# Expert items 1 to 6 of TensorE's program written out instead of looped

## The chip, the cores and the metric

One core of one Trainium2 chip runs the whole program. The metric is the device time of one execution in microseconds (us). The time before is the median of three runs, 1470.57 us (1469.07 to 1472.14).

## What is computed

The reference is a small model on 256 tokens of width 1024: two layers of a convolution and gating mixer, the first followed by a dense SwiGLU, the second by a mixture of 8 SwiGLU experts (each 1024 to 2816 to 1024, two experts a token), then an attention block with two kinds of attention. The change lies in the experts:

```python
D_MODEL = 1024; D_FF = 2816; N_EXPERTS = 8; TOP_K = 2

def swiglu(h, wg, wu, wd):
    return jnp.einsum('...f,fd->...d', jax.nn.silu(h @ wg) * (h @ wu), wd)

def moe_swiglu(h, router, wg, wu, wd):
    ...
    logits = jnp.einsum('td,de->te', ht, router).astype(jnp.float32)
    top_vals, top_idx = lax.top_k(logits, TOP_K)
    gates = jax.nn.softmax(top_vals, axis=-1)
    ...
    for e in range(N_EXPERTS):
        out = out + dense_gate[:, e:e + 1] * swiglu(ht, wg[e], wu[e], wd[e])
```

The expert weights are float32: 3 x 1024 x 2816 x 4 bytes, 34.6 MB for one expert, 277 MB for all eight.

## The kernel before, in words

Every engine runs one instruction stream of its own, and the streams are tied by semaphores. The program is the mixer of layer 0, the dense SwiGLU, the mixer of layer 1, the router, then the **items**, and then the attention block. An item is up to 96 tokens of one expert. There are at least 8, numbered 0 to 7 (`NE` is 8), and up to five more when an expert is crowded; the number of the last one is known only on the chip (`last`, read from `plan`).

An item's weights are cut into 24 chunks. Chunks 0 to 15 are gate and up weights: 0 to 7 are 1.57 MB each, 8 to 15 are 1.31 MB each. Chunks 16 to 23 are the down weights, 1.57 MB each, the last two 1.05 MB. They land in a ring of 8 slots (`ering`, `ESLOTS` is 8). SyncE issues their DMAs (`load_expert`, line 452): the DMA of chunk c waits until TensorE is done with chunk c - 8 (semaphore `w_used`), since that is the one whose slot it takes. TensorE waits for a chunk by the semaphore `e_landed` of its slot. So up to seven whole chunks can be on their way or landed while TensorE works on one.

TensorE multiplies by all of a chunk in one go: the tokens (`xe`) or the hidden values (`eT`) are the stationary side, 32 columns of them at a time, one after the other on four column strips (`by_strips`, line 2701), and the weights stream through. In the trace, a `LDWEIGHTS` and a `MATMUL` record stand for each half of a product in float32. After chunk 8 and chunk 16 TensorE turns the hidden values of one half (`turn_hidden`, line 2687), and after chunk 16 also the tokens of the next item (`turn_tokens`, line 2680). VectorE and ScalarE do the activation, the product with the up part and the copies, with waits that count up by fixed steps each item. ScalarE writes an item's result to `ys` with three DMAs, and SyncE reads the next item's tokens from `xs` with one.

On each of the four engines the items are written alike: item 0 by itself, then a hardware loop over items 1 to 6, then a branch over a second, conditional body for items beyond the eighth, then the last item by itself. Inside the loop the item number i is a register, so the values that the waits compare with are worked out in registers (`landed(i, j)`, `FREED * i` and the like). The function `item` tells item 0 from the looped ones by `isinstance(i, int)`: item 0 waits for other semaphores on its first four chunks, reads `last`, and turns the places of the last item's tokens.

Of the kernel before, what the change touches and what calls it, by code (L numbers as in the profile page):

```python
# [34 lines left out]
NE = 8  # L35
# [91 lines left out]
def model_program(nc, a, out):  # L127
# [313 lines left out]
    def landed(i, j):  # L441

        slot = range(j % ESLOTS, FFN_CHUNKS, ESLOTS)
        before = 16 * MOE0 // RAWS if slot[0] < RAWS else 0
        return before + 16 * sum(LANDINGS[n] for n in slot if n <= j) + i * (16 * sum(LANDINGS[n] for n in slot))
# [705 lines left out]
    def second_tensor(pe, n_items, norm_transposes, last_item):  # L1151
# [22 lines left out]
        def meta_low(c):  # L1174
            pe.wait_ge(blo_made, c + 1)
            _, wl = wide(c)
            for k in range(4):
                kt = 4 * c + k
                mm = nc.tensor.matmul(ps[0:META, 3, 0:W2], xTm_hi[:, kt, T:TM], wl[:, k, :], start=False, stop=kt == KT - 1)
            return mm  # L1180
# [352 lines left out]
    with nc.Block() as block:  # L1533
# [807 lines left out]
        def _(pe):  # L2341
# [333 lines left out]
            def turn_tokens(i):  # L2675
                pe.wait_ge(xg_landed, 16 * (i + 1))
                for part in range(2):
                    for kk in range(4):
                        k = 4 * part + kk
                        mm = nc.tensor.transpose(ps[:, part, kk * CAP:kk * CAP + CAP], xg[0:CAP, k * P:k * P + P], ident[0:CAP, 0:CAP])  # L2680
                    mm.then_inc(tp_filled, 1)

            def turn_hidden(i, piece):
                pe.wait_ge(emult_made, MULTS * i + (7 if piece else 3))
                for jb in range(3):
                    for t in range(TOKS):
                        mm = nc.tensor.transpose(ps[:, 3 + jb, t * P:t * P + P], eh[piece][:, t, jb * P:jb * P + P], ident)  # L2687
                    mm.then_inc(tp_filled, 1)

            def turn_last_places():  # L2690
                pe.wait_ge(pick_made, 2 + TOKS * NB)
                for t in range(TOKS):
                    for b in range(NB):
                        first = (2 * (t % 2) + b) * P
                        mm = nc.tensor.transpose(ps[:, 6 + t // 2, first:first + P], pick_last[:, t, b, :], ident)
                mm.then_inc(g0_filled, 1)
# [7 lines left out]
            def gate_or_up(j):  # L2704
                piece, up = j // 8, j // 4 % 2
                n = WIDE[piece]
                w = slot_view(ering, j % ESLOTS, 2, STRIPS * n)
                for k in range(2):
                    kt = 2 * (j % 4) + k
                    for t in range(TOKS):  # L2710
                        mm = by_strips(lambda rows: ps[rows, 3 * up + t, 0:n], xe[:, kt, STRIP * t:STRIP * t + STRIP], w[:, k, :], n,
                                       kt == 0, kt == KT - 1)
                return mm

            def down(j, t, n, tile):
                w = slot_view(ering, j % ESLOTS, len(DOWN_TILES[j - 16]), D)
                first = t % 2 * DOWN_N
                return by_strips(lambda rows: ps[rows, 6 + t // 2, first:first + DOWN_N], eT[:, tile, STRIP * t:STRIP * t + STRIP],
                                 w[:, n, :], DOWN_N, tile == 0 and t != 1, tile == FT - 1)

            def item(i, last=False):
                first = isinstance(i, int)
                for j in range(16):
                    if first and j < 4:
                        pe.wait_ge(g0_hi if j % 2 else g0_freed, j // 2 + 1)
                    if j == 0 and not first:
                        pe.wait_ge(tp_freed, FREED * i)
                        pe.wait_ge(esilu_made, 7 * i)
                    if j == 8:
                        pe.wait_ge(esilu_made, 7 * i + 3)  # L2730
                    if j == 12:
                        pe.wait_ge(tp_freed, FREED * i + 3)
                        if first:
                            read_last()
                    pe.wait_ge(e_landed[j % ESLOTS], landed(i, j))
                    gate_or_up(j).then_inc(w_used, 1)
                    if j == 8:
                        turn_hidden(i, 0)
                        if first:
                            turn_last_places()  # L2740
                for j in range(16, FFN_CHUNKS):
                    if j == 16 and first:
                        pe.wait_ge(g0_freed, 4)
                    elif j == 16:
                        pe.wait_ge(eo_made, 2 * i)
                    if j == 20:
                        pe.wait_ge(tp_freed, FREED * i + 7)
                    pe.wait_ge(e_landed[j % ESLOTS], landed(i, j))
                    if last and j == FFN_CHUNKS - 1:
                        for t in range(TOKS):  # L2750
                            for n, tile in enumerate(DOWN_TILES[j - 16]):
                                mm = down(j, t, n, tile)
                            if t:
                                mm.then_inc(w_used if t == TOKS - 1 else acc_ready, 1)
                        return
                    for n, tile in enumerate(DOWN_TILES[j - 16]):
                        for t in range(TOKS):
                            mm = down(j, t, n, tile)
                    mm.then_inc(w_used, 1)
                    if j == 16:  # L2760
                        turn_hidden(i, 1)
                        if not last:
                            turn_tokens(i)
# [3 lines left out]
            def read_last():  # L2767
                pe.wait_ge(routed, 1)
                last_of.append(pe.value_load(plan[0:1, LAST_COL:LAST_COL + 1], min_val=NE - 1, max_val=ITEMS - 1))

            pe.wait_ge(pick_made, 2)
            for p in range(4):
                gather(p)
            item(0)
            with pe.Fori(1, NE - 1) as i:
                item(i)
            last = last_of[0]
            n_items = last + 1
            with pe.If(last > NE - 1):
                with pe.Fori(NE - 1, ITEMS - 1) as i:  # L2780
                    with pe.If(i < last):
                        item(i)
# [38 lines left out]
```

## Time and profile before

| what | us |
|---|---|
| median of three runs | 1470.57 |
| the profiled execution, its own time | 1468.36 |
| its span in the trace | 1466.5 |
| TensorE busy in it | 1393.0 (95%) |
| VectorE, ScalarE, GpSimd busy | 514.8, 384.8, 75.2 |

The span runs from the first to the last instruction in the trace; the 1.9 us between it and the execution's time lie around it. The eight items take roughly from 407 to 1187 us. The rows of the section below come from this one execution. In a chain or a timeline, the first number is the start in us from the span's start, the second the length. A granted clock (PEclk) of 1.00 is TensorE at 2.4 GHz, 0.50 is 1.2 GHz.

### The profile page before, as it was taken

What the parts mean: (1) busy time and instruction counts of PE and PEld (TensorE: products, weight loads), DVE (VectorE), ACT (ScalarE), POOL (GpSimd) and SP (SyncE); (2) the same over time, 40 slices, a digit from 0 to 9 for tenths busy, and PEclk for the clock granted to TensorE, in tenths of its full rate; (3) what the DMA queues carried; (4) which work ended last, traced back from release to release, by engine and by line L of the source; (5) the groups of instructions that cost most, each with busy time, mean ns of one, the idle gap of its engine ahead of it and who ended that gap; (6) DMA issues with size and microseconds to landing.
All of it is one profiled execution on the core that took longest, in us unless ns stands there. A gap on an engine that the chain in (4) does not pass through costs nothing.

```text
span 1466.5 us, 33021 instructions
## 1 busy us (share of the span) xinstructions
PE 1393.0 (95%) x14972; PEld 960.6 (66%) x14972; DVE 514.8 (35%) x836; ACT 384.8 (26%) x527; POOL 75.2 (5%) x130
## 2 busy tenths in 40 slices
PE   6999999999999999798997997998989989999998
PEld 6879998897855656245354453452554559788896
DVE  6975555389522001010010010010101154656665
ACT  5664443346400000000000000000000045656653
POOL 3400000043010000000000000000000010000000
PEclk9999999999899999899998998998999999999999
DMA  9569974454779999999999999999999955343341
GB/s 320 162 219 328 294 230 171 144 178 152 312 297 357 382 390 348 382 358 345 370 351 366 343 347 378 341 374 336 344 353 403 353 205 169 104 143 117 116 169 61
DMA packets 122585, 407.35 MB, mean 278 GB/s; under 512 B 7430, under 2 KB 35958, under 8 KB 122436
## 3 DMA queue, kind: packets, MB, share of 16 engines
q1 hardware_dynamic: 114192, 389.57, 74.7%
q0 software_dynamic: 5408, 12.58, 2.6%
q8 instruction: 133, 2.18, 0.6%
q10 hardware_dynamic: 2836, 2.88, 0.6%
q14 instruction: 16, 0.13, 0.0%
HBM read 396.78 MB, written 16.12 MB: 282 GB/s over the span
## 4 chain that ended last, share of the span: by engine, by line
PE 84%; DVE 8%; issue 4%; ACT 2%; DMA 1%; SPq 0%; DVEq 0%; ACTq 0%
PE ps L2701 48%; PE ps L516 6%; PE ps L518 6%; PE ps L517 6%; DVE yT L2027 3%; PE ps L1198 1%; DVE low L506 1%; PE ps L1200 1%; PE ps L1199 1%; PE ps L2687 1%; PE ps L2386 1%; DMA rawb<-in_w_in 1%; PE ps L1407 1%; PE ps L1405 1%; PE ps L1406 1%
## 5 line engine op out<-in xcount | busy, mean ns | idle before, releaser
L2701 PE MATMUL ps<-ering,xe 128*32 128x384 f32 (+1 forms) x6144 | 481.4, 470 | 43.4 <-issue 43.4
L2701 PEld LDWEIGHTS ps<-ering,xe 128*32 128x32 f32 x6144 | 213.8, 112 | 306.0 <-issue 186.6
L2701 PE MATMUL ps<-ering,eT 128*32 128x256 f32 x4224 | 233.0, 379 | 2.0 <-issue 2.0
L2203 DVE TENSOR_TENSOR eh<-eh,ps 128x384 f32<-128x384 f32 (+1 forms) x48 | 22.1, 517 | 580.3 <-PE ps L2701 580.3
L2701 PEld LDWEIGHTS ps<-ering,eT 128*32 128x32 f32 x4224 | 146.5, 110 | 84.9 <-issue 3.4
L506 DVE TENSOR_TENSOR low<-raw,high 128x2048 fp32r<-128x2048 f32 (+3 forms) x48 | 128.9, 2686 | 61.6 <-ACT high L501 60.4
L501 ACT ACTIVATE high<-raw 128x2048 fp32r<-128x2048 f32 (+3 forms) x47 | 105.5, 2246 | 91.0 <-PE ps L518 76.1
L516 PE MATMUL ps<-high,xT_hi 128*128 128x352 f32 (+1 forms) x368 | 128.2, 348 | 1.2 <-DVE xT_lo L2109 1.2
L518 PE MATMUL ps<-high,xT_lo 128*128 128x352 f32 (+1 forms) x368 | 127.1, 345 | 0.0
L1880 ACT ACTIVATE eh<-ps 128x384 f32<-128x384 f32 (+1 forms) x48 | 18.9, 466 | 411.8 <-PE ps L2701 411.8
L517 PE MATMUL ps<-low,xT_hi 128*128 128x352 f32 (+1 forms) x368 | 126.9, 345 | 0.0
L903 DVE TENSOR_TENSOR lowb<-rawb,highb 128x2048 fp32r<-128x2048 f32 x35 | 80.0, 2289 | 47.7 <-ACT highb L681 47.6
L681 ACT ACTIVATE highb<-rawb 128x2048 fp32r<-128x2048 f32 x35 | 66.9, 1911 | 84.8 <-DMA rawb<-in_w_in 38.2
L1890 ACT ACTIVATE eo<-ps 128x512 f32<-128x512 f32 x8 | 4.8, 596 | 298.5 <-PE ps L2701 298.5
L516 PEld LDWEIGHTS ps<-high,xT_hi 128*128 128x128 f32 x368 | 69.1, 188 | 7.7 <-DVE xT_lo L2109 2.2
L518 PEld LDWEIGHTS ps<-high,xT_lo 128*128 128x128 f32 x368 | 69.2, 188 | 5.1
L517 PEld LDWEIGHTS ps<-low,xT_hi 128*128 128x128 f32 x368 | 69.2, 188 | 4.8
L1198 PE MATMUL ps<-xTm_hi,highb 128*128 128x256 f32 x224 | 64.2, 286 | 0.0
L1199 PE MATMUL ps<-xTm_lo,highb 128*128 128x256 f32 x224 | 62.6, 279 | 0.0
L1200 PE MATMUL ps<-xTm_hi,lowb 128*128 128x256 f32 x224 | 62.5, 279 | 0.0
L2027 DVE SCALAR_TENSOR_TENSOR yT<-cT,cols,yT 128x256 f32<-128x256 f32 x120 | 48.8, 480 | 0.0
L1198 PEld LDWEIGHTS ps<-xTm_hi,highb 128*128 128x128 f32 x224 | 42.1, 188 | 1.3 <-issue 1.2
(436 smaller groups left out, 1670.5 us busy)
## 6 DMA issues: line engine op xcount, KB each, us to landing
ering<-in_moe_wg SPq DMA_DIRECT2D x32, 1536.0 KB, 15.7
ering<-in_moe_wu SPq DMA_DIRECT2D x32, 1536.0 KB, 17.6
ering<-in_moe_wd SPq DMA_DIRECT2D x32, 1536.0 KB, 11.9
ering<-in_moe_wg SPq DMA_DIRECT2D x32, 1280.0 KB, 9.2
ering<-in_moe_wu SPq DMA_DIRECT2D x32, 1280.0 KB, 8.5
rawb<-in_w_in SPq DMA_DIRECT2D x25, 1024.0 KB, 5.1
ering<-in_moe_wd SPq DMA_DIRECT2D x24, 1024.0 KB, 17.1
raw<-in_w_in SPq DMA_DIRECT2D x16, 1024.0 KB, 9.1
```

The costliest lines, as they stand in the source:

```text
L501: nc.scalar.activation(high[:, c % SPLITS, 0:n], raw[:, c % RAWS, 0:n], ACT.Copy).then_inc(hi_made, 1)
L506: nc.vector.tensor_tensor(low[:, c % SPLITS, 0:n], raw[:, c % RAWS, 0:n], f(high[:, c % SPLITS, 0:n]), ALU.subtract).then_inc(lo_made, 1)
L516: nc.tensor.matmul(out, xh, wh, start=first, stop=False)
L517: nc.tensor.matmul(out, xh, wl, start=False, stop=False)
L518: return nc.tensor.matmul(out, xl, wh, start=False, stop=last)
L681: nc.scalar.activation(highb[:, c % SPLITS, :], rawb[:, c % RAWSB, :], ACT.Copy).then_inc(bhi_made, 1)
L903: nc.vector.tensor_tensor(lowb[:, c % SPLITS, :], rawb[:, c % RAWSB, :], f(highb[:, c % SPLITS, :]), ALU.subtract).then_inc(blo_made, 1)
L1198: nc.tensor.matmul(o, wh[:, k, chans], yT_hi[:, kt, :], start=kt == 0 and t == 0, stop=False, **mmx)
L1199: nc.tensor.matmul(o, wh[:, k, chans], yT_lo[:, kt, :], start=False, stop=False, **mmx)
L1200: mm = nc.tensor.matmul(o, wl[:, k, chans], yT_hi[:, kt, :], start=False, stop=kt == KT - 1, **mmx)
L2027: ins = nc.vector.scalar_tensor_tensor(yT[:, t, :], src, w, yT[:, t, :], ALU.mult, ALU.add)
L2701: mm = nc.tensor.matmul(out_of(rows), tokens, weights[:, n * s:n * s + n], start=begins, stop=ends, skip_group_check=True)
```

## The change

TensorE's loop over items 1 to 6 becomes a Python loop, so that six bodies stand one behind the other in its program with plain constants in their waits. The test for "first" is narrowed, since now six more items are called with an int. VectorE, ScalarE and SyncE keep their hardware loops, and the conditional second loop of TensorE stays as it is.

```diff
             def item(i, last=False):
-                first = isinstance(i, int)
+                first = isinstance(i, int) and i == 0
                 for j in range(16):
...
             item(0)
-            with pe.Fori(1, NE - 1) as i:
+            for i in range(1, NE - 1):
                 item(i)
             last = last_of[0]
```

```order
 L2680 MATMUL ps<-small,xg 128x96 x8
 L2701 MATMUL ps<-ering,eT 32x256 x228
-L2775 UNCONDITIONAL_BRANCH
-L2775 ISA
-L2728 REGISTER_ALU
-L2735 ISA
-L2701 MATMUL ps<-ering,xe 32x384 x96
-L2735 ISA
-L2701 MATMUL ps<-ering,xe 32x384 x48
-L2735 REGISTER_ALU
-L2701 MATMUL ps<-ering,xe 32x384 x48
```

The branch into the loop's head and the sequencer's register work at the head are gone; the same 192 products follow the 228 of item 0 directly (next block).

At the loop's end, the closing branch goes and another item begins in its place:

```order
-L2775 REGISTER_ALU
-L2775 COMPARE_AND_BRANCH
+L2701 MATMUL ps<-ering,eT 32x256 x228
+L2701 MATMUL ps<-ering,xe 32x384 x192
+L2701 MATMUL ps<-ering,xe 32x320 x24
+L2687 MATMUL ps<-small_68,eh_113 128x128 x9
+L2701 MATMUL ps<-ering,xe 32x320 x168
+L2701 MATMUL ps<-ering,eT 32x256 x36
```

The compare and branch that closed the loop stands nowhere in the new program; the branch at L2779, over the conditional body, stays where it was, behind item 6. On SyncE and ScalarE no instruction differs between the two programs.

## Rows read from the trace of the kernel before

**Rows 1.** The page: TensorE's busy time, and the span in 40 slices.

```profile
PE 1393.0 (95%) x14972; PEld 960.6 (66%) x14972; DVE 514.8 (35%) x836; ACT 384.8 (26%) x527; POOL 75.2 (5%) x130
...
PEclk9999999999899999899998998998999999999999
DMA  9569974454779999999999999999999955343341
GB/s 320 162 219 328 294 230 171 144 178 152 312 297 357 382 390 348 382 358 345 370 351 366 343 347 378 341 374 336 344 353 403 353 205 169 104 143 117 116 169 61
```

**Rows 2.** Chain of waits in time, 500 to 1150 us: start, length, what.

```profile
577.58 0.72 issue
...
587.57 5.08 issue
592.65 2.76 PE ps L2701 x10
595.41 2.50 issue
597.91 35.79 PE ps L2701 x419
...
1090.80 5.29 issue
1096.09 5.22 PE ps L2701 x33
```

**Rows 3.** Waits: SyncE's queue, 500 to 1190 us; TensorE, 500 to 1150 (total, times, longest).

```profile
SPq L452 <- PE ps L2701: 544.1, 159, 16.2
...
PE ps L2701 <- issue: 45.1, 14, 5.3
```

**Rows 4.** Timeline of TensorE, the first products of item 1.

```profile
497.50 0.49 PE L2701 MATMUL ps<-ering,xe 128*32 128x384 f32 x2
```

**Rows 5.** Windows at two edges: PE, PEld, DVE, ACT, POOL busy, PEclk, DMA, GB/s.

```profile
587.60:602.10 14.50, 6.95 (x38) 1.94 (x42) 0.00 (x0) 0.88 (x2) 0.00 (x0) 0.65 1.02 414
...
1090.80:1100.70 9.90, 4.61 (x32) 1.51 (x33) 0.00 (x0) 0.87 (x2) 0.00 (x0) 0.66 1.02 413
```

**Rows 6.** DMA view, 350 to 1170 us: the instruction queue, tokens, results.

```profile
q8 instruction: 98, 1.61, 0.8%
...
xg<-xs SPq DMA_DIRECT2D x7, 384.0 KB, 11.4
ys<-eo ACTq DMA_DIRECT2D x21, 128.0 KB
```

**Rows 7.** Windows of an item's length or so, same columns as rows 5.

```profile
483.00:580.00 97.00, 96.28 (x1461) 57.96 (x1455) 7.18 (x16) 3.46 (x9) 0.00 (x0) 1.00 1.02 380
498.00:587.60 89.60, 88.85 (x1320) 50.78 (x1312) 7.18 (x16) 3.46 (x9) 0.00 (x0) 1.00 1.02 377
...
677.00:776.00 99.00, 90.62 (x1309) 46.58 (x1305) 7.18 (x16) 3.46 (x9) 0.00 (x0) 0.98 1.01 366
...
1081.00:1174.00 93.00, 87.30 (x1250) 43.21 (x1252) 11.21 (x18) 3.46 (x9) 5.04 (x8) 0.96 0.98 382
```

**Rows 8.** Time from issue to landing, expert chunks issued 537 to 588 us.

```profile
DMA to landing us min/median/max: 13.8/20.9/24.5
```

**Rows 9.** The same, chunks issued 990 to 1041 us.

```profile
DMA to landing us min/median/max: 5.7/7.5/10.8
```

**Rows 10.** Windows within item 1 and its end, same columns as rows 5.

```profile
498.00:540.00 42.00, 42.00 (x543) 23.54 (x539) 2.97 (x6) 2.13 (x5) 0.00 (x0) 1.00 1.02 415
...
567.00:579.00 12.00, 11.28 (x213) 6.71 (x205) 0.00 (x0) 0.00 (x0) 0.00 (x0) 1.00 1.02 246
```

**Rows 11.** The DMA of item 2's chunk 1, alone in the window 565 to 566 us.

```profile
L452 SPq DMA_DIRECT2D ering<-in_moe_wg x1: 372/372/372, 565.9 to 565.9; - x1
...
DMA to landing us min/median/max: 20.9/20.9/20.9
```

**Rows 12.** Chain of waits, 985 to 1190 us: what follows the last item.

```profile
1175.35 12.28 DMA rawb<-in_w_in
...
1189.53 0.59 ACT eo L1890
```

## The prediction

> **What bounds the kernel now.** I read the page first. TensorE is busy 95% of the span, so the end is set by what it does and where it stands still. But in slices 13 to 32, the items, the DMA engines are busy nine tenths or more as well and move 336 to 403 GB/s, and the granted clock dips to 8 tenths in several slices [rows 1]. So two resources are near their limits, and a pause taken out of one can run into the other.
>
> The chain of waits on TensorE shows the pauses. At 587.57, where item 1 ends and item 2 begins, TensorE stands for 5.08 us, does ten matmuls, stands another 2.50 us, and goes on; the wait is put down to "issue", to nothing that the profile can name, not to a DMA or an engine [rows 2]. The same pair comes behind items 2, 3, 4 and 5, and behind item 6 a single pause of 5.29 us [rows 2]. Together these are 45.1 us of "issue" in 14 pieces, TensorE's only wait in that stretch [rows 3]. All the long ones sit where the loop branches back or is left; at the entry of item 1 there is none, its first products begin at 497.50 [rows 4]. I read them as the fetch of TensorE's code after a jump: one item is some 2,630 instructions (1320 matmuls and 1312 weight loads in its 89.6 us [rows 7]), and the second pause, ten matmuls in, has the look of the next piece of code being late too.
>
> The pauses also cost clock. In the 14.5 us from 587.6 the mean granted clock is 0.65, against 1.00 over item 1 [rows 5, 7]: TensorE falls from 2.4 to 1.2 GHz after standing, and comes back after some microseconds of work.
>
> The Trainium skill, "Runtime: NRT & Kernel Launch", section "Instruction fetch mechanics", says that instructions are fetched in order ahead of use and that a taken branch to a place outside what is held makes the engine wait for a fetch. The trace agrees, with 5.08 us at the branch and none at the straight entry of item 1.
>
> Last, how far ahead the weights are. SyncE's queue waits for TensorE to free a slot for 544.1 us in all [rows 3], which looks as if DMA had time to spare. The time to landing says otherwise: 20.9 us in the median for chunks issued from 537 to 588 us, 24.5 at most [rows 8], and only 7.5 for those issued from 990 to 1041 [rows 9]. An item of 24 chunks takes TensorE about 90 us, 3.8 a chunk, so seven chunks of lead are some 26 us, and that is all there is. In item 1, which had no pause in front of it, the DMA was falling behind; after each pause it had caught up. The pauses give the DMA time.
>
> **What the change takes away.** Five taken branches, behind items 1 to 5. From the end of item 1 (587.57) to the end of item 6 (1090.80) are 503.2 us for five items, 100.6 us each [rows 2]. Item 1 itself, without a pause ahead, took 587.57 - 497.50 = 90.1 us [rows 2, 4]. The difference, 10.5 us an edge, is 5.1 + 2.5 = 7.6 us of pauses and 2.9 us for the lower clock. If nothing else held, five items would take 450.5 us, and **52.7 us** would go.
>
> **What is late next.** The weights. An item needs 34.6 MB of them, 0.39 MB of tokens and 3 x 0.13 MB of results [rows 6], and 1.61 MB of instructions over about eight items, 0.2 each [rows 6]: 35.6 MB. The DMA does 415 GB/s through gate and up chunks but only 246 GB/s at the end of an item, where the down weights land in strips [rows 10]. Over windows of about one item with many chunks under way it did 380, 377 and 382 GB/s, and 366 in a window where it was less far behind [rows 7]. A period of the DMA alone is therefore 35.6 / 0.382 = 93.2 us at best, 35.6 / 0.366 = 97.3 us at worst. Both are above TensorE's 90.1. In the changed kernel the DMA has all eight slots to work on, which speaks for the upper rates, but TensorE's waits come where landing is slowest, which the windows may flatter: their edges cut through chunks that have partly landed. I take the middle of 380 and 366, 373 GB/s, so 95.4 us.
>
> How much lead is left at 587.57: item 2's chunk 1 was issued at 565.9 and landed 20.9 us later, at 586.8 [rows 11]. Without a pause TensorE wants it one chunk after 587.57, at 591.4. The lead is 4.6 us and lasts for less than one item (95.4 - 90.1 = 5.3). From then on, an item takes the DMA's time, and item 7's chunk 1 lands five periods after item 2's, just when it is wanted. The five items take 5 x 95.4 - 4.6 = 472.4 us instead of 503.2: **30.8 us less.** With 93.2 it is 41.8, with 97.3 it is 21.3.
>
> **What I cost at nothing.** The register work and the branch into the loop: before, they showed as no pause at item 1's entry [rows 4]; below that there is only the gap's own size. Straight code crosses fetches too; in item 1 that showed once, 0.72 us [rows 2]. At one such pause for each of five items that would be 3.6 us if TensorE were the bound; waiting for weights, it hides them, so zero, with 3.6 as the far end. The branch behind item 6 stays. It cost 5.29 us and a clock of 0.66 for a while [rows 2, 5]; its place among the fetched pieces of code shifts, so a second pause of 2.5 us may appear, as behind the others [rows 2], or the present one shrink, by 5.3 at most. I take no change. Behind it item 7 goes on as before: the pause gives the DMA some 8 us, and item 7's window needed 382 GB/s [rows 7], which is what the DMA can do. After item 7 the attention block's first weights are on the chain, issued at 1175.35 [rows 12]. They are issued when TensorE frees slots, so they move with it; should the backlog reach them, their landing slips by no more than the lead lost, 4.6 us. None is taken, both ends go to the range.
>
> **The sum.** Profiled execution: 1468.4 - 30.8 = 1437.6 us. The median of the runs is 2.2 us above that execution, so **1440 us**, rounded.
>
> **The rivals.**
> *The DMA keeps up* (TensorE remains the bound). For it: 415 GB/s over 42 us [rows 10]; if the slow end of an item is smoothed by a deep queue, 35.6 / 0.415 = 85.8 us, under 90.1. Against: in item 1 the queue was deep and the end ran at 246 all the same. Time: 1470.6 - 52.7 = 1418 us. Chance 0.13.
>
> *The DMA's limit is lower than I think* and the pauses were mostly cover for it. For it: with the pauses, slices 18 to 29, items 2 to 6, drew only 336 to 378 GB/s [rows 1]. A rate of 358 GB/s would make the period 99.4 us, five items 492.4, the gain 10.8, the time 1460 us. Against: 380 GB/s over 97 us [rows 7]; the lower slices have landing times down to 5.7 us [rows 9], so the DMA was then waiting for slots. The Trainium skill, "DMA: Bandwidth & Descriptors", section "Specifications", gives 358 GB/s as the HBM limit of a core and 435 as the fabric's ceiling; by the first this rival would be right, and the trace, with one core at work, is above it. Chance 0.17.
>
> *Slower: the clock.* Starved of weights, TensorE would wait at the slow end of every item, fall to 1.2 GHz, and pay more than the loop did. One fall costs 2.9 us, as at an edge. An item is longer than before once it has 10.5 / 2.9 = 3.6 falls; with five, it takes 104.6 us, five items 20 us more than before, 1490 us. For it: at 246 GB/s [rows 10] a last chunk of 1.05 MB takes 4.3 us to land, and TensorE two thirds of 3.8, 2.5 us, to use, which leaves gaps of 1.8 us. Against: the pause of 0.72 us left the clock of item 1 at 1.00 [rows 7], the falls came after 5 us; and a slow TensorE no longer waits for the DMA, so it fills its time again and recovers. The Trainium skill, "TensorE: Matmul & The Clock Gate", section "HAM oscillation — how this bites in real kernels", describes such a kernel, in which each wait for weights let the clock drop again; no run here shows that. Chance 0.04.
>
> *It does not do what it says*: the long pauses are not of the branch but of something each item start has, and stay. Against: item 1's start has none. 1470.6 us, chance 0.03.
>
> **How the numbers follow.** The forecast, period 93.2 to 97.3 us, has 0.63, its own range 1429 to 1450. Lower, the DMA-keeps-up case adds 0.13 down to 1418; upward, half of the lower-limit case lies between 1450 and 1460. The range is 1418 to 1460. About 0.2% (3 us) is what a measurement can tell from no change. Faster by more than that: forecast, keeps-up and lower-limit cases, 0.93. Within: 0.03. Slower: 0.04.
>
> **What would show it.** At the edges of items 1 to 5 no "issue" pause over 1 us, and no dip in clock there. Behind item 6 a pause of about 5 us still. Item 2 some 90 us long, items 4 to 6 some 95 us. TensorE waiting for landed chunks at the end of items, a few microseconds an item. Landing times of 20 us and more in the median throughout, and 370 to 380 GB/s in every item. I am wrong if items 4 to 6 take 90 us (the DMA keeps up), if they take 99 or more (its limit is lower), or if the clock over them is under 0.9 (the clock).

## The result, and the profile after

The median went from 1470.23 us (7 runs, 1466.16 to 1472.14) to **1458.26 us** (7 runs, 1455.77 to 1464.85): a ratio of 0.9931, 95% interval 0.9909 to 0.9953. That is 12 us less, clear of what a measurement can tell from no change, inside the range of the prediction, and 39% of the 30.8 us that it forecast.

The page of the changed kernel, the lines that answer to [rows 1]:

```profile
PE 1385.4 (95%) x14972; PEld 960.7 (66%) x14972; DVE 514.8 (35%) x836; ACT 384.2 (26%) x527; POOL 75.0 (5%) x130
...
PEclk9999999999899999999999999999999989999999
DMA  9569864454879999999999999999999945243341
GB/s 321 163 223 327 295 227 173 144 174 155 315 296 365 379 390 336 415 376 336 407 314 372 382 288 413 375 321 407 327 381 377 319 165 179 96 144 116 116 174 58
```

The dips of the clock inside the items are gone, and yet TensorE's share is still 95%. The chain of waits of the changed kernel, from 480 to 700 us, shows the edges of items 1 (at 586.4) and 2 (at 677.1); it answers to [rows 2]:

```profile
560.27 16.10 PE ps L2701 x295
576.37 1.04 issue
577.41 43.20 PE ps L2701 x593
...
671.00 1.49 issue
672.49 4.62 PE ps L2701 x77
```

From 577.41 on TensorE works through the place at which it stood for 5.08 and 2.50 us before. Small pauses of the straight code remain, 1.04 and 1.49 us here, over the 1 us that the prediction allowed at an edge. TensorE's waits from 490 to 1090 us (total, times, longest) answer to [rows 3]:

```profile
PE ps L2701 <- DMA ering<-in_moe_wd: 21.7, 12, 2.8
PE ps L2701 <- issue: 7.6, 3, 5.1
PE ps L2701 <- DMA ering<-in_moe_wu: 4.7, 15, 0.4
PE ps L2701 <- DMA ering<-in_moe_wg: 3.4, 6, 0.9
PE ps L2680 <- DMA xg<-xs: 2.0, 3, 0.8
```

The 45.1 us of "issue" became 7.6, of which 5.1 is the pause behind item 6 that was to stay. In their place stand 31.8 us of waits for transfers, in 36 pieces, none longer than 2.8 us. The windows of items 1 to 6 (columns as in [rows 5]):

```profile
496.50:586.40 89.90, 88.86 (x1329) 49.05 (x1322) 7.18 (x16) 3.44 (x9) 0.00 (x0) 1.00 1.02 373
586.40:677.10 90.70, 89.18 (x1323) 54.90 (x1314) 7.18 (x16) 3.44 (x9) 0.00 (x0) 1.00 1.02 367
677.10:779.60 102.50, 93.91 (x1326) 46.28 (x1330) 7.18 (x16) 3.45 (x9) 0.00 (x0) 0.97 1.02 361
779.60:878.60 99.00, 91.99 (x1322) 44.79 (x1314) 7.18 (x16) 3.45 (x9) 0.00 (x0) 0.98 1.02 357
878.60:977.70 99.10, 90.93 (x1322) 44.91 (x1322) 7.18 (x16) 3.45 (x9) 0.00 (x0) 1.00 1.02 365
977.70:1077.00 99.30, 90.94 (x1322) 45.70 (x1322) 7.19 (x16) 3.44 (x9) 0.00 (x0) 1.00 1.01 367
```

Item 2 still takes TensorE's time, 90.7 us: the lead is used up in it. From item 3 on an item takes 99 us and more, hardly less than the 100.6 with the pauses, and the DMA engines are busy throughout, yet move only 357 to 367 GB/s. The times to landing, chunks issued from 677 to 728 us and from 728 to 777 (against 7.5 in the median in [rows 9]):

```profile
DMA to landing us min/median/max: 21.4/23.4/29.4
...
DMA to landing us min/median/max: 15.9/26.6/31.8
```

Within item 3 the windows say where the rate is lost (columns as before); they answer to [rows 10]:

```profile
677.10:732.00 54.90, 52.57 (x681) 23.07 (x685) 2.97 (x6) 3.45 (x9) 0.00 (x0) 1.00 1.02 410
732.00:750.00 18.00, 17.24 (x280) 9.88 (x273) 4.21 (x10) 0.00 (x0) 0.00 (x0) 1.00 1.03 358
750.00:774.00 24.00, 19.66 (x328) 11.14 (x320) 0.00 (x0) 0.00 (x0) 0.00 (x0) 0.93 1.03 245
774.00:800.00 26.00, 24.44 (x296) 9.46 (x300) 0.00 (x0) 2.13 (x5) 0.00 (x0) 0.93 1.01 410
```

The stretch at 245 GB/s, with the DMA engines as busy as elsewhere, is 24 us long; in item 1 of the kernel before, a window of 12 us showed 246. It is where the last down chunks and the first chunks of the next item are under way.

So the change did what it says, and the expected gain went into waits for weights. Two questions were open: is it only the weights, and why do they come at 99 us an item when 35.6 MB at 415 GB/s would take 86?

### The profile page after: what moved, and what is told of

Read it like the earlier page. It is cut to its first block, busy times and chain, and to the rows that moved or that the text cites. A ratio compares the mean times of both kernels' runs of the same rounds, so it can differ in the third digit from the quotient of the medians.

```text
span 1461.4 us, 32936 instructions
## 1 busy us (share of the span) xinstructions
PE 1385.4 (95%) x14972; PEld 960.7 (66%) x14972; DVE 514.8 (35%) x836; ACT 384.2 (26%) x527; POOL 75.0 (5%) x130
## 4 chain that ended last, share of the span: by engine, by line
PE 61%; DMA 21%; DVE 7%; SPq 7%; issue 2%; ACT 2%; ACTq 0%; DVEq 0%; POOL 0%; POOLq 0%
PE ps L2701 24%; DMA ering<-in_moe_wu 8%; PE ps L516 6%; PE ps L518 6%; SPq L452 6%; PE ps L517 6%; DMA ering<-in_moe_wd 5%; DMA ering<-in_moe_wg 4%; DVE yT L2027 3%; DMA ys<-eo 2%; PE ps L1198 2%; PE ps L1200 2%; PE ps L1199 2%; DVE low L506 1%; DMA rawb<-in_w_in 1%
## 5 line engine op out<-in xcount | busy, mean ns | idle before, releaser
L2701 PE MATMUL ps<-ering,xe 128*32 128x384 f32 (+1 forms) x6144 | 464.1, 461 | 13.2 <-issue 5.1
L2701 PE MATMUL ps<-ering,eT 128*32 128x256 f32 x4224 | 240.9, 385 | 25.9 <-DMA ering<-in_moe_wd 22.4
## 6 DMA issues: line engine op xcount, KB each, us to landing
ering<-in_moe_wd SPq DMA_DIRECT2D x32, 1536.0 KB, 21.9
```

Source lines behind the costliest of these rows:

```text
L2701: mm = nc.tensor.matmul(out_of(rows), tokens, weights[:, n * s:n * s + n], start=begins, stop=ends, skip_group_check=True)
```

## The experiments

Each experiment's ratio is to runs of the kernel before made beside it, with medians of 1469.4 to 1469.6 us. The straight kernel (the changed one) was not run again beside them; its 1458.26 us and its ratio of 0.9931 (0.9909 to 0.9953) come from the runs above. Where an edit changes how many DMAs load a chunk or store a result, the counts that the waits compare with change along; those lines are left out of the diffs.

### Halved loads, looped and straight

Both kernels with half of chunks 0 to 7 left out in items 1 to 7:

```diff
-            rows(slot_view(ering, s, 2, width), (wg_v, wu_v)[up][e, :, k:k + 2, piece * PIECE0:piece * PIECE0 + width])
+            count = 2 if piece or (isinstance(e, int) and e == 0) else 1
+            rows(slot_view(ering, s, 2, width)[:, 0:count, :],
+                 (wg_v, wu_v)[up][e, :, k:k + count, piece * PIECE0:piece * PIECE0 + width])
```

> The looped kernel with only half of chunks 0 to 7 loaded in items 1 to 7 (0.79 MB each instead of 1.57; the other half of each slot holds old data, so the expert products of those chunks are not the reference's). 34.6 MB an item become 28.3. If the loads bind the changed kernel: here, where the branch pauses bind, the items still take 100 to 101 us each, and the whole is 1470 us within 4. Rival (the loads also bind the looped kernel in part): 3 to 5 us an item shorter, below 1455 us.

> The same halved loads in the kernel with the items written out. If the landing of weights is what ate the gain: items 2 to 6 take TensorE's 90 us instead of 99, TensorE waits for no chunk, and the whole is 45 to 53 us under the looped kernel with halved loads, 1417 to 1425 us. Rival (the straight code itself is slower, by late fetches or by the clock): the items stay at 97 us or more, and the whole over 1450 us.

Measured: looped 1441.71 us (1438.46 to 1444.96; ratio to the kernel before 0.9812, 0.9776 to 0.9849), straight 1408.90 us (1407.78 to 1410.02; 0.9589, 0.9562 to 0.9616). In the straight kernel the items take 88.5 to 90.5 us at a clock of 1.00, with no wait for a chunk. These are the windows of its items 2 and 3:

```profile
584.40:672.90 88.50, 88.50 (x1326) 44.46 (x1322) 7.18 (x16) 3.45 (x9) 0.00 (x0) 1.00 0.95 330
672.90:761.60 88.70, 88.70 (x1329) 44.32 (x1325) 7.18 (x16) 3.45 (x9) 0.00 (x0) 1.00 0.95 330
```

With the landing relieved, the straight code runs at TensorE's own pace; the weights ate the gain. The straight kernel came out below the 1417 to 1425 us expected, and 33 us under the looped one instead of 45 to 53, since the looped one got faster too. That one missed its expectation, and the rival's sign came true: 28 us less, 20 of them in items 2 to 6, which take 96.5 us each instead of 100.6. Where the other 8 went was not taken apart. No wait for a chunk was removed there, since there was none. What shrank is the pause at the branch, in its chain of waits:

```profile
585.11 3.62 issue
588.73 1.47 PE ps L2703 x10
590.21 1.32 issue
...
680.23 3.95 issue
684.18 2.76 PE ps L2703 x10
686.95 0.17 issue
```

3.6 to 4.0 us and then 0.2 to 1.7 us, instead of 4.9 to 5.1 and 2.4 to 2.7: with fewer loads beside it (306 to 331 GB/s during the first pause instead of some 410), the late code comes sooner. The trace of the kernel before has the instruction queue's packets in both pauses, two in the first (587.6 to 592.7 us) and one in the second (595.4 to 598), 16 KB each:

```profile
q8 instruction: 2, 0.03, 2.9%
...
q8 instruction: 1, 0.02, 2.6%
```

All this fits a pause that is a transfer of code, sharing the DMA engines with the weights, so that the loop's price depends on them.

### The end chunk in one DMA, straight and looped

Chunk 23 holds the last 64 rows of each of the four strips, and is loaded by two DMAs, each onto 64 of the 128 partitions. Here it is one DMA of the same bytes:

```diff
-            ends = wd_v[e, PIECE0:, :].rearrange("(t u q) n -> u q t n", t=2, u=2)
-            for u in range(2):
-                rows(slot_view(ering, s, 2, D)[2 * STRIP * u:2 * STRIP * u + REST, :, :], ends[u, 2 * P:, :, :])
+            tiles(0, FF - 2 * P, 2)
```

> Straight kernel, chunk 23 loaded by one DMA onto all 128 partitions (the last 256 rows of the down weights, other rows than the reference's; same bytes) instead of two DMAs onto 64 partitions each. Theory A, second part (the loads onto a part of the partitions crowd the ways into them and slow what is beside them: GB/s falls to 250 at the end of an item): the rate there rises to over 380, items 3 to 6 take 94 to 95 us, the whole 16 to 20 us less, about 1440 us. Theory B (bytes alone): no change, 1458 within 4.

> The looped kernel with chunk 23 loaded by one DMA onto 128 partitions (other rows than the reference's, same bytes), the twin of the straight kernel with that load, which took 1406 us. If the loop's price is the branch pauses and the clock behind them, shown in full only where the loads don't bind: items 2 to 6 take 97 to 99 us (88.5 and 9 to 10 at the edge), the whole 1443 to 1455 us, so that straight against loop is worth 40 to 48 us here and was worth 12 with the split load. Rival (most of the 52 us that the whole load gave the straight kernel it gives the looped one too): under 1430 us.

Measured: straight **1406.07 us** (1403.04 to 1408.18; 0.9569, 0.9544 to 0.9595), far below the 1440 expected; looped 1464.07 us (1462.78 to 1465.62; 0.9968, 0.9958 to 0.9979), above the 1443 to 1455 expected. The windows of items 2 to 4 of the straight one:

```profile
583.70:672.20 88.50, 88.50 (x1326) 44.46 (x1322) 7.18 (x16) 3.44 (x9) 0.00 (x0) 1.00 1.02 398
672.20:760.70 88.50, 88.50 (x1326) 44.45 (x1322) 7.18 (x16) 3.44 (x9) 0.00 (x0) 1.00 1.02 402
760.70:849.20 88.50, 88.50 (x1326) 44.56 (x1322) 7.18 (x16) 3.44 (x9) 0.00 (x0) 1.00 1.02 400
```

About 400 GB/s over whole items, and TensorE never waits for a chunk: its period of 88.5 us is the bound, and this is the case "the DMA keeps up" of the prediction. The looped one keeps its edges, here in its chain of waits:

```profile
584.21 4.96 issue
589.18 2.76 PE ps L2699 x10
591.94 2.44 issue
...
682.43 5.07 issue
687.50 2.76 PE ps L2699 x10
690.26 2.71 issue
```

Its items take 98.2, 101.2, 100.2, 101.2 and 100.1 us, most of them more than the 97 to 99 expected: 88.5 us and some 11.7 for the edge and the clock behind it. **Writing out the items is worth 58 us with the whole load and 12 with the split one.** One part of the kernel held down what another could give. The two changes together bring 64 us, apart 12 and 5.

### The result stored by strips

ScalarE's three stores of an item have a target whose first dimension is 4, the strips. Here they are four stores of 32 partitions:

```diff
-                    for t in range(TOKS):
-                        act.dma_start(ys_v[i - 1, STRIP * t:STRIP * t + STRIP, :].rearrange("p (s n) -> s p n", s=STRIPS), eo[:, t, :]).then_inc(eo_landed, 16)
+                    for s in range(STRIPS):
+                        act.dma_start(ys_v[i - 1, :, DOWN_N * s:DOWN_N * (s + 1)].rearrange("(t p) n -> p t n", t=TOKS),
+                                      eo[STRIP * s:STRIP * s + STRIP, :, :]).then_inc(eo_landed, 16)
```

> Straight kernel, the item's result stored by four DMAs of 32 partitions each instead of three of 128 partitions whose target's first dimension is 4. Theory A (a chunk counts as landed when the slowest of the DMA engines is through; the stores put all their packets on four of the sixteen, which then land every chunk late, 4.4 us instead of 3.8 for chunks 3 to 7): chunks 3 to 7 land 3.8 us apart, items 3 to 6 take 96 us instead of 99, the whole about 12 us less, 1446 us. Theory B (the bound is the sum of bytes at some 360 GB/s, whatever engine carries them): no change, 1458 within 4.

Measured: 1451.57 us (1450.68 to 1454.71; 0.9887, 0.9863 to 0.9910), 7 us less than the straight kernel and not the 12 expected (the intervals of the two ratios just touch); items 3 to 6 take 100.3, 95.7, 99.3 and 94.7 us, 97.5 in the mean instead of 100.0. Chunks 3 to 7 land 4.0 us apart in the mean of these items, instead of 4.4. Theory B falls, since the bytes are the same. That the stores go over four engines shows in the DMA view of one item (583 to 671 us): queue 10 has 396 packets in the changed kernel and 448 here.

```profile
q10 hardware_dynamic: 396, 0.39, 1.3%
```

```profile
q10 hardware_dynamic: 448, 0.39, 1.3%
```

384 of them carry data; the rest are the marks with which each engine reports its share, 12 for three stores before, 64 for four now: 4 engines a store against 16. The Trainium skill, "DMA: Bandwidth & Descriptors", section "Why a DMA increments its semaphore by 16 and not by 1", says that the number of engines is the largest up to 16 that divides the slowest dimension of both sides. The trace agrees, 4 where that dimension is 4.

### Quarters by turns, and two queues

Two other ways to load chunk 23. In four DMAs, by turns from the lower and the upper half:

```diff
-            for u in range(2):
-                rows(slot_view(ering, s, 2, D)[2 * STRIP * u:2 * STRIP * u + REST, :, :], ends[u, 2 * P:, :, :])
+            for half in range(2):
+                for u in range(2):
+                    at = 2 * STRIP * u + STRIP * half
+                    rows(slot_view(ering, s, 2, D)[at:at + STRIP, :, :],
+                         ends[u, 2 * P + STRIP * half:2 * P + STRIP * half + STRIP, :, :])
```

> Straight kernel, chunk 23 correct, in four DMAs of 32 partitions each, taken by turns from the lower and the upper half of the partitions, instead of two of 64. Theory (a DMA onto 64 partitions has all sixteen engines write through half of the ways into the memory): by turns, engines that run apart would mix the halves, and the slow stretch at the end of an item gets faster; 1425 to 1445 us. Rival (small partial DMAs crowd whatever their order): 1458 us or more.

And with the second half on ScalarE's queue, behind the last activation of each item:

```diff
-            for u in range(2):
-                rows(slot_view(ering, s, 2, D)[2 * STRIP * u:2 * STRIP * u + REST, :, :], ends[u, 2 * P:, :, :])
+            rows(slot_view(ering, s, 2, D)[0:REST, :, :], ends[0, 2 * P:, :, :])
...
+            def second_ends(i, e):
+                s = (FFN_CHUNKS - 1) % ESLOTS
+                ends = wd_v[e, PIECE0:, :].rearrange("(t u q) n -> u q t n", t=2, u=2)
+                act.wait_ge(w_used, chunk(i, FFN_CHUNKS - ESLOTS))
+                act.dma_start(slot_view(ering, s, 2, D)[2 * STRIP:2 * STRIP + REST, :, :], ends[1, 2 * P:, :, :]).then_inc(e_landed[s], 16)
```

> Straight kernel, chunk 23 correct, its second half (64 partitions) issued on ScalarE's queue instead of SyncE's. It does not stand behind the other seven chunks there and is mixed packet by packet with loads onto all partitions. Theory as for the quarters: less crowding, 1430 to 1450 us. Rival: no change, 1458 us, or slower where ScalarE's wait for the slot delays the storing of a result.

Measured: quarters 1450.10 us (1448.20 to 1451.66; 0.9872, 0.9852 to 0.9891), 8 us less than the straight kernel, between the 1445 us of the theory and the 1458 of its rival; two queues 1458.08 us (1448.65 to 1461.35; 0.9908, 0.9878 to 0.9939), not to be told from no change. Neither the order nor the queue brings the 52 us that one DMA onto 128 partitions brings. It isn't the number of DMAs in a chunk either: four were no slower here than two, and chunks 20 and 21 are two DMAs each in every kernel, the 1406 us one too, but onto all partitions.

### A hint for the loop's branch

```diff
-            with pe.Fori(1, NE - 1) as i:
+            with nc.Fori(1, NE - 1, engines=[pe.engine], hint_back_edge=True) as i:
```

Measured: 1460.87 us (1456.99 to 1467.92; 0.9946, 0.9929 to 0.9962). The time is in the expected place, but the edges are not as expected. Its chain of waits:

```profile
587.18 4.21 issue
591.39 2.12 PE ps L2701 x9
593.51 3.26 issue
...
687.77 3.40 issue
691.17 2.12 PE ps L2701 x9
693.29 3.23 issue
```

The first pause falls from about 5.0 us to between 2.5 and 4.2, the second grows from about 2.5 us to between 3.2 and 3.5. The loads had been expected to become the bound, and did not: TensorE waits for no chunk in this run. That a hint about the fetch alone moves the pauses speaks for the fetch as their cause; why it takes away only a part is open. Nothing was tried on when the hinted code is asked for.

### Everything that the loads need, with the whole reference computed

The end rows of two neighbouring strips can be made 128 rows in a row, if the odd strips give up their first 64 columns instead of their last:

```diff
-            return PIECE0 + WIDE[1] * n
+            return PIECE0 + WIDE[1] * n + REST * (n % 2)
...
-            ends = wd_v[e, PIECE0:, :].rearrange("(t u q) n -> u q t n", t=2, u=2)
-            for u in range(2):
-                rows(slot_view(ering, s, 2, D)[2 * STRIP * u:2 * STRIP * u + REST, :, :], ends[u, 2 * P:, :, :])
+            ends = wd_v[e, PIECE0:, :].rearrange("(t r) n -> r t n", t=2)
+            rows(slot_view(ering, s, 2, D), ends[2 * P:3 * P, :, :])
...
+                def at(rows):
+                    return REST if piece and rows.start // STRIP % 2 == 0 else 0
...
-                        mm = by_strips(lambda rows: ps[rows, 3 * up + t, 0:n], xe[:, kt, STRIP * t:STRIP * t + STRIP], w[:, k, :], n,
+                        mm = by_strips(lambda rows: ps[rows, 3 * up + t, at(rows):at(rows) + n], xe[:, kt, STRIP * t:STRIP * t + STRIP], w[:, k, :], n,
```

Even strips write their 320 outputs from column 64 on, odd strips from 0; the activations read columns 64 to 383 and, for the ends, 0 to 63. No instruction is added.

> Straight kernel in which chunk 23 is one DMA onto 128 partitions and the whole reference is computed: odd strips give the first 64 of their 320 columns to the last tiles instead of the last 64, so that the ends of two neighbouring strips are 128 rows in a row. No instruction is added on TensorE. As in the run that loaded other rows in one DMA: items of 88.5 us, TensorE waits for no chunk until item 6, 1406 us within 4. Rival (what that run gained came from the place of its rows in memory, not from the shape of the DMA): over 1425 us.

The second kernel adds the stores by strips, the third loads the tokens onto 128 partitions instead of 96:

```diff
-                sp.dma_start(xg[0:CAP, :], xs_v[i + 1, :, :]).then_inc(xg_landed, 16)
+                sp.dma_start(xg[:, :], xs[bass.ds((i + 1) * CAP, P), :]).then_inc(xg_landed, 16)
```

> The same, with the results stored by four DMAs of 32 partitions. Theory A: the spread between the first and the last engine's share of a chunk no longer grows from item to item, chunks 3 to 7 land 3.8 us apart throughout, the loads run ahead of TensorE; since TensorE already bounds the items, the whole is at most 3 us less than without it, 1403 to 1406 us. Rival: the four extra stores an item cost something where item 7 begins, over 1408 us.

> The same, and the tokens loaded onto 128 partitions instead of 96 (32 rows more, which nothing uses). If loads onto a part of the partitions crowd: the interval of chunk 17 falls from 7 to under 5.5 us; hidden by the lead, so no change in the whole beyond 2 us, 1402 to 1406 us. Rival: the extra bytes cost, over 1408 us.

> The looped kernel with all three changes of the loads and stores, the twin of the run before. If the branch pauses are all that the loop costs: items 2 to 6 take 98 to 101 us, the whole 1455 to 1465 us, so that writing out the items is worth 52 to 58 us here. Rival (the relieved DMA engines also shorten the fetch pauses, as with the halved loads): pauses of 4 us instead of 5, the whole 1440 to 1455 us.

| kernel | median us | range | ratio to the kernel before (95%) |
|---|---|---|---|
| straight, ends in one DMA | 1405.73 | 1404.05 to 1406.49 | 0.9566 (0.9547 to 0.9585) |
| and stores by strips | 1402.26 | 1401.79 to 1406.85 | 0.9553 (0.9529 to 0.9577) |
| and tokens onto 128 partitions | 1405.92 | 1403.92 to 1406.27 | 0.9564 (0.9546 to 0.9583) |
| looped, with all three | 1466.01 | 1463.17 to 1467.87 | 0.9977 (0.9965 to 0.9989) |

The first meets the run with other rows (1406.07 us), so it was the shape of the DMA, not the place of its rows. This is the version that beats both kernels. The stores and the tokens on top make no difference that these runs can tell: TensorE is the bound. The interval at which chunk 17 lands behind chunk 16 was 5.3 to 7.0 us with the stores by strips and 4.2 to 4.7 with the tokens on 128 partitions, as expected (items 2 to 6). The first kernel's waits of TensorE, 490 to 1090 us, and its windows of items 3 and 6:

```profile
PE ps L2700 <- issue: 5.0, 1, 5.0
PE ps L2686 <- DVE eh L2202: 2.1, 1, 2.1
```

```profile
672.20:760.70 88.50, 88.50 (x1330) 44.47 (x1326) 7.18 (x16) 3.46 (x10) 0.00 (x0) 1.00 1.02 399
...
937.60:1026.10 88.50, 88.02 (x1318) 44.07 (x1310) 7.18 (x16) 3.44 (x10) 0.00 (x0) 1.00 1.02 401
```

Only the pause behind item 6 and one wait of 2.1 us for VectorE are left. The looped twin lies 60 us above the straight one, a little over the 52 to 58 expected, and its first pauses are 5.1 to 5.5 us long, so its rival with shorter ones did not come true.

Each of a chunk's sixteen shares has its landing in the trace. How far apart the first and the last of them are, in us, for chunk 4:

| kernel | item 3 | item 6 |
|---|---|---|
| before | 4.3 | 3.6 |
| straight | 9.8 | 13.3 |
| straight, stores by strips | 8.1 | 15.3 |
| straight, ends in one DMA (whole reference) | 4.4 | 9.5 |
| and stores by strips | 4.6 | 8.5 |
| and tokens onto 128 partitions | 2.7 | 3.2 |

TensorE can begin a chunk only when its last share is there. In the straight kernel the engines drift apart from item to item, until the first is 13 us ahead of the last; in the looped kernel before, the spread at these two items is about 4 us. The ends in one DMA narrow it, and the tokens on top of them bring it down to 3.2 us at item 6. The stores by strips had been expected to stop its growth, and did not: with the ends in one DMA it is 8.5 us at item 6, and in the straight kernel 15.3, though that kernel got 7 us shorter. A wide spread alone does not make an item slow: with the ends in one DMA it is 9.5 us at item 6, and the item takes 88.5.

Where the time goes shows in how long the last shares of a stretch of chunks take to come, in us, mean of items 3 to 6:

| kernel | chunks 0 to 2 | 3 to 7 | 8 to 15 | 16 to 23 | all 24 |
|---|---|---|---|---|---|
| straight | 11.4 | 21.9 | 26.7 | 40.0 | 100.0 |
| straight, stores by strips | 11.6 | 19.9 | 26.1 | 39.7 | 97.3 |
| straight, ends in one DMA (whole reference) | 11.3 | 20.9 | 27.4 | 30.6 | 90.2 |

Of the 9.8 us an item between the first and the last row, 9.4 lie in the down chunks, where the stretch at 245 GB/s is; the stores on four engines are worth some 2 us in chunks 3 to 7. The last row is near TensorE's own 88.5 us, so the loads alone may be faster still.

## Why the prediction was right or wrong

**What bounds before; the pauses are late code.** Right, as far as the runs can tell. Undoing only the branch took away both pauses at the edges of items 1 to 5 and nearly all of the clock's dips, the halved loads shortened them, and the hint moved them. Its price was put at 10.5 us an edge, 52.7 in all, if nothing else held; with the end chunk whole it showed as 11.7 an edge and 58 in all.

**What is late next.** The weights, right, and where: TensorE's new waits are on landed chunks, most on the down weights. The lead of 4.6 us and its end within item 2 were right in kind: item 2 took 90.7 us.

**The size of the DMA's period: the step that failed.** The prediction took 35.6 MB at 373 GB/s, 95.4 us, between ends of 93.2 and 97.3. Measured: 99.1 us in the mean of items 4 to 6, outside those ends. In its own formula 5 x 99.1 - 4.6 = 490.9 us instead of 472.4; measured from the end of item 1 to the end of item 6, 1077.0 - 586.4 = 490.6. That one term accounts for the whole miss. Over items 4 to 6 the rate was 363 GB/s in the mean, and 35.6 MB at that rate are 98.1 us; the rest is bytes, since the DMA engines moved 36.0 MB an item there. The 373 was the middle of 366 and of the 380 from a window over item 1 [rows 7], and item 1 is not the steady state: the straight kernel itself does 373 GB/s over item 1, then 367, 361 and 357, and its slow stretch at 245 GB/s is 24 us long in item 3, where the window over item 1 held 12 us of it [rows 10]. Why it is longer there was not tested. The sentence that the windows may flatter was there, the allowance for it too small. The prediction also took the 246 GB/s as what such loads cost, and not as the one thing in the DMA's period that could be removed.

**The rival with a lower limit** gave 1460 us and has the time, and its sign, items 4 to 6 at 99 us or more, came true; but its reason is not the one: 358 GB/s is not a limit here, since the same bytes came at 400 GB/s once chunk 23 was one DMA. The 358 GB/s that the Trainium skill, "DMA: Bandwidth & Descriptors", section "Specifications", gives as the HBM limit of a core would have led to the right time for the wrong cause. **The rival that the DMA keeps up** was right for a kernel one edit away, 1406 us.

**The clock.** Over item 3, whose waits are up to 2.3 us long, it was 0.97; over items 5 and 6, with waits of up to 2.8 us, it was 1.00. The slower rival didn't come true: the short waits cost little clock.

**What was put at nothing.** The pause behind item 6 stayed at 5.1 us; item 7 took 98.2 us against 96.0 before, 2.2 us more, which the prediction had left to the range; the smaller lead may be the cause, no run was made on it. The small pauses of the straight code, 1.0 and 1.5 us, are hidden by the waits that follow.

## What to carry to other kernels

Before you price the removal of a stall, ask what uses it: a ring whose loads were catching up during each stall bounds the gain by the loads' own period. Read that period from a stretch in which the loads alone set the pace, and look inside it for its slowest part, since a window that holds little of that part flatters the rate. Look at the shapes of the few DMAs that differ from the rest: one target with a first dimension of 4, or two DMAs onto half of the partitions, can hold back a stream that is 97% well shaped. When an edit brings far less than its stall was worth, try it again with the next bound lifted: here 12 us became 58.

## What the runs showed of the hardware that was not expected

- 1.05 MB an item, 3% of its bytes, cost the straight kernel 52 us over the items because it was loaded as two DMAs onto 64 partitions each: while they were under way, the DMA engines as a whole slowed to 245 GB/s, for 24 us in item 3, and the 6 KB packets of the other loads took 447 ns in the median there (750 to 774 us) instead of 235 (680 to 730 us). The Trainium skill, "DMA: Bandwidth & Descriptors", section "Rules for kernel authors", advises one 128-partition transfer instead of two onto disjoint halves, since both halves use all sixteen engines; this trace agrees, and shows a price well beyond the two DMAs themselves.
- TensorE's pause behind a taken branch, put down to the fetch of its code, was 4.9 to 5.9 us with the DMA engines full, and 3.6 to 4.0 us with them at 306 to 331 GB/s.
- A hint for the branch took away only 1 to 2.5 us of the first pause and added about 0.8 to the second.
